# Moving one of six weight loads in the block-product pairs of a decoder layer: up's two-row sum block behind the last blocks of gate and up

## The chip, the cores and the metric

The kernel runs on one core of one Trainium2 chip. The metric is device time in microseconds (us) of one execution, lower is better. A core has TensorE (PE in the profile, with its weight loads as PEld), VectorE (DVE), ScalarE (ACT), GpSimd (POOL), and SyncE (SP), which here only issues transfers. All transfers of the core share 16 DMA engines.

## The reference, cut to what matters

One decoder layer on 512 tokens of width 1024: a half-step SwiGLU feed-forward network (FFN), a token mixing step (a pooling branch beside sliding-window attention, merged by gates), and a second half-step SwiGLU FFN. All in float32.

```python
def swiglu(x, w_gate, w_up, w_down):
    return (jax.nn.silu(x @ w_gate) * (x @ w_up)) @ w_down

h = h + 0.5 * swiglu(rmsnorm(h, ffn1_norm), ffn1_w_gate, ffn1_w_up, ffn1_w_down)
...
h = h + 0.5 * swiglu(rmsnorm(h, ffn2_norm), ffn2_w_gate, ffn2_w_up, ffn2_w_down)
```

`w_gate` and `w_up` are 1024 x 2816, which is 22 column tiles of 128. The change lies in how the products `x @ w_gate` and `x @ w_up` of the two FFNs get their weights.

## The kernel before, in words

**Precision.** Every product is made of three passes over weights and moving data that are split in a high part (rounded to the format that TensorE reads, by ACT) and a low part (the rest, by a subtraction on DVE or POOL): high by high, high by low, low by high. They are lines 544 to 546 for whole tiles and 650 to 652 for blocks.

**Plain tiles and pairs.** The first 8 column tiles of FFN 1 and the first 6 of FFN 2 are computed plainly. The other 14 and 16 are taken two at a time, in 7 and 8 pairs (`PAIRS`). A pair uses a Strassen-Winograd scheme: gate and up each take 7 block products where plain blocks would take 8, so 14 products a pair (`STEPS`). A product is 12 matmuls of 128 columns of weights by 256 tokens, followed by one count on the semaphore `product`. `done(n, i, pos)` is the count that says that product number `pos` (0 to 13) of pair `i` of FFN `n` has ended.

**What a pair needs.** For gate and for up alike:

- `a1` (512 KB, a row of two blocks; `gate_a`, `up_a` in the profile, line 418),
- `s31` (two rows of weights in one 512 KB transfer, line 423), to which POOL adds another 512 KB by an accumulating transfer of its own (`add_units`, line 1463). The result is the two-row sum block. It has two buffers, so it is fetched two pairs ahead. `gate_s`, `up_s` in the profile,
- `a22` (256 KB; also `gate_a`, `up_a`, line 428).

The profile leaves buffer names out: `up_s` is up's `s31`, `s2` or `s4`, and `up_a` is its `a1` or `a22`.

**What is made of them.** DVE adds `s2` and `s4` from `s31` and `a1` (`weight_sums`, lines 1670 and 1672), ACT rounds each block to its high part (lines 1043 to 1057), DVE subtracts the low parts of `a1`, `s2` and `s31` (lines 1678, 1682, 1686), and POOL those of `s4` and `a22` (`late_lows`, lines 1468 and 1471). DVE also adds partial sums of the product banks in PSUM (`add_part`, line 1802), which TensorE's last two products of the pair, `a22(0)` and `a22(1)`, positions 12 and 13, wait for.

**Order.** Each engine runs its own list in the order in which it is written; the semaphores alone tie the lists. SP's list for a pair is `pairs`, with a wait on `product` in front of each load. POOL's list for a pair is the four `late_lows` (gate's s4, gate's a22, up's s4, up's a22), then the two `add_units` of the pair after next, gate's and up's; each `add_units` first waits until the `s31` load that it adds to has landed. DVE's list for a pair is in `pair`: two partial sums, then for the next pair `weight_sums` and `low_a1` of gate (behind product 4), the same of up (behind product 6), `low_s2` of gate, then partial sum, `low_s31` of gate, and three more partial sums.

```python
def add_units(n, i, k, w):
    g = first_pair(n) + i
    pool.wait_ge(w["s31_landed"][buffer(g)], 16 * fills(g))
    pool.dma_start(w["s31"][buffer(g)][:, :], weights_in[D_PAIRS[n] + 4 * i + k + 2, :, :],
                   accum_op=ALU.add).then_inc(w["s31_summed"][buffer(g)], 16)
...
late_lows(first_pair(n) + i, gate_w)
late_lows(first_pair(n) + i, up_w)
if i + 2 < PAIRS[n]:
    add_units(n, i + 2, 0, gate_w)
    add_units(n, i + 2, 1, up_w)
```

Of the kernel before, what the change touches and what calls it, by code (L numbers as in the profile page):

```python
# [55 lines left out]
PAIRS = tuple((FT - p) // 2 for p in PLAIN)  # L56
# [68 lines left out]
def layer_kernel(nc, x_in, consts_in, params_in, poolw_in, weights_in, out):  # L125
    ctx = ExitStack()
    with ctx:
# [4 lines left out]
        def sem(name):  # L132
            return ctx.enter_context(nc.semaphore(name))
# [37 lines left out]
        def blocks(name, a, s31, s2, a22, s4, high_a, high_s31, high_s2, high_a22, high_s4):  # L171

            wide, one = [P, UNIT], [P, UNIT // 2]
            return dict(
                a=put(name + "_a1", wide, a), a_l=put(name + "_a1_low", wide, a, F32R),
                s31=[put(f"{name}_s31_{q}", wide, o) for q, o in enumerate(s31)],
                s31_l=[put(f"{name}_s31_low_{q}", wide, o, F32R) for q, o in enumerate(s31)],
                s2=put(name + "_s2", one, s2), s2_l=put(name + "_s2_low", one, s2, F32R),
                a22=put(name + "_a22", one, a22), a22_l=put(name + "_a22_low", one, a22, F32R),
                s4=[put(f"{name}_s4_{q}", one, o) for q, o in enumerate(s4)],  # L180
                s4_l=[put(f"{name}_s4_low_{q}", one, o, F32R) for q, o in enumerate(s4)],
                a_h=put(name + "_a1_high", wide, high_a, F32R), s31_h=put(name + "_s31_high", wide, high_s31, F32R),
                s2_h=put(name + "_s2_high", one, high_s2, F32R), a22_h=put(name + "_a22_high", one, high_a22, F32R),
                s4_h=put(name + "_s4_high", one, high_s4, F32R),
                a_landed=sem(name + "_a1_landed"), s31_landed=[sem(f"{name}_s31_landed{q}") for q in range(2)],
                s31_summed=[sem(f"{name}_s31_summed{q}") for q in range(2)], a22_landed=sem(name + "_a22_landed"),
                summed=sem(name + "_s2_s4_summed"), high=sem(name + "_blocks_high"),
                low=sem(name + "_blocks_low"), late=sem(name + "_late_blocks_low"))
# [5 lines left out]
        up_w = blocks("up", m, (m + 4096, m + 12288), m + 8192, m + 10240, (M_UP_S4, M_UP_S4 + 2048),  # L194
                      M_HIGH, M_HIGH + 4096, M_HIGH + 8192, M_HIGH + 10240, M_HIGH + 12288)
# [83 lines left out]
        product = sem("product_done")  # L279
# [75 lines left out]
        def first_pair(n):  # L355

            return PAIRS[0] if n else 0

        def buffer(g):

            return (g if g < PAIRS[0] else g - PAIRS[0]) % 2
# [7 lines left out]
        def done(n, i, pos):  # L369

            return STEPS * (first_pair(n) + i) + pos + 1
# [30 lines left out]
        def _(sp):  # L402
# [14 lines left out]
            def load_a1(n, i, k, w):  # L417
                sp.dma_start(w["a"][:, :], weights_in[D_PAIRS[n] + 4 * i + k, :, :]).then_inc(w["a_landed"], 16)

            def load_s31(n, i, k, w):  # L420
                d = D_PAIRS[n] + 4 * i + k
                b = buffer(first_pair(n) + i)
                sp.dma_start(w["s31"][b][:, :].rearrange("p (a n) -> p a n", a=2),
                             weights_in[d:d + 3:2, :, 0:UNIT // 2].rearrange("a p n -> p a n")
                             ).then_inc(w["s31_landed"][b], 16)

            def load_a22(n, i, k, w):
                sp.dma_start(w["a22"][:, :], weights_in[D_PAIRS[n] + 4 * i + k + 2, :, UNIT // 2:UNIT]
                             ).then_inc(w["a22_landed"], 16)
# [18 lines left out]
            def pairs(n):  # L448

                for i in range(PAIRS[n]):  # L450
                    if i + 1 < PAIRS[n]:
                        sp.wait_ge(product, done(n, i, 1))
                        load_a1(n, i + 1, 0, gate_w)
                        sp.wait_ge(product, done(n, i, 3))
                        load_a1(n, i + 1, 1, up_w)
                    if i + 2 < PAIRS[n]:
                        sp.wait_ge(product, done(n, i, 8))
                        load_s31(n, i + 2, 0, gate_w)
                        sp.wait_ge(product, done(n, i, 10))
                        load_s31(n, i + 2, 1, up_w)  # L460
                    if i + 1 < PAIRS[n]:
                        sp.wait_ge(product, done(n, i, 12))
                        load_a22(n, i + 1, 0, gate_w)
                        sp.wait_ge(product, done(n, i, 13))
                        load_a22(n, i + 1, 1, up_w)

            def first_down(n, u):

                last = PAIRS[n] - 1
                sp.wait_ge(product, done(n, last, 3))  # L470
                load(u)
                sp.wait_ge(product, done(n, last, 10))
                load(u + 1)
                sp.wait_ge(product, done(n, last, 13))
                load(u + 2)
                load(u + 3)
# [30 lines left out]
            for u in range(SLOTS, U_DN1):  # L507
                load_used(u)
                if u == SLOTS + 4:
                    gate_prologue(0)  # L510
            up_prologue(0, U_DN1 - SLOTS)
            pairs(0)
            first_down(0, U_DN1)
            for u in range(U_DN1 + SLOTS, U_POOL + SLOTS):
# [5 lines left out]
            for u in range(U_GU2 + SLOTS + 1, U_DN2):  # L520
                load_used(u)
            up_prologue(1, U_DN2 - SLOTS)
            pairs(1)
            first_down(1, U_DN2)
            for u in range(U_DN2 + SLOTS, UNITS):
# [1711 lines left out]
```

## Time and profile before

| what | value |
|---|---|
| median of 3 runs | 1045.54 us (1045.41 to 1046.3) |
| the profiled execution's own time | 1046.29 us |
| its span, first to last instruction | 1044.5 us |
| PE busy | 1037.8 us (99%) |
| PEld busy | 904.9 us (87%) |
| DVE busy | 648.8 us (62%) |
| ACT busy | 469.2 us (45%) |
| POOL busy | 407.6 us (39%) |
| granted TensorE clock | 1.0 |
| read from HBM | 121.76 MB |

The profile is of one execution. Its times are us from the span's start unless marked ns. A row of the timeline gives an instruction's start, how long it took, its engine, its line in the kernel, its operation and its tiles (written, then read), and in brackets the idle time of the engine before it and what ended it. A row of a transfer queue gives packets, MB and the share of the 16 DMA engines' time; a row of single transfers gives the tile, the queue that issues, the count, the size and the us from issue to landing. Transfers of POOL's queue are the accumulating ones. The pairs of FFN 1 lie between 95 and 237 us, those of FFN 2 between 758 and 922 us.

### The profile page before, as it was taken

To read this page: it belongs to the slowest core of one execution; us is meant where nothing else is said; L and a number is where in the kernel's file an instruction comes from. 1 tells how busy PE (TensorE), PEld (TensorE's weight loads), DVE (VectorE), ACT (ScalarE), POOL (GpSimd) and SP (SyncE) were. 2 spreads that over 40 slices of the span, in tenths; PEclk is the share of its full clock that TensorE was granted. 3 is DMA by queue.
4 is the path that set the end of the run, shared out by engine and by line. 5 is a ranking of instruction groups with operands and counts; after the bars stand their busy time and mean duration, and the time that the engine had idled before them with its cause. 6 is when DMAs were issued, how large, how long until landed. Compare 5 with 4: busy or idle time off the path is not lost.

```text
span 1044.5 us, 15205 instructions
## 1 busy us (share of the span) xinstructions
PE 1037.8 (99%) x5940; PEld 904.9 (87%) x5940; DVE 648.8 (62%) x997; ACT 469.2 (45%) x810; POOL 407.6 (39%) x229
## 2 busy tenths in 40 slices
PE   9999999999999999999999999999999999999998
PEld 7888999998888888887777888888899999988887
DVE  6997776669240378426677656679996777594101
ACT  6453554545231334247676643434345554453210
POOL 1302334325444443344455545434324233254441
PEclk9999999999999999999999999999999999999999
DMA  6735677613233432222111122325367577232332
GB/s 212 215 102 133 165 188 195 179 53 120 92 100 101 141 122 84 87 81 81 61 61 60 56 70 97 101 87 146 111 163 193 157 183 195 80 105 98 101 101 101
DMA packets 42292, 124.81 MB, mean 119 GB/s; under 512 B 4336, under 2 KB 5616, under 8 KB 42224
## 3 DMA queue, kind: packets, MB, share of 16 engines
q1 hardware_dynamic: 37616, 107.85, 31.2%
q0 software_dynamic: 4320, 15.73, 8.9%
q8 instruction: 46, 0.75, 0.3%
q10 hardware_dynamic: 288, 0.29, 0.1%
q14 instruction: 22, 0.18, 0.0%
HBM read 121.76 MB, written 2.10 MB: 119 GB/s over the span
## 4 chain that ended last, share of the span: by engine, by line
PE 95%; DVE 2%; DMA 1%; issue 1%; ACT 1%; SPq 0%; DVEq 0%; ACTq 0%
PE psum L544 21%; PE psum L545 21%; PE psum L546 21%; PE psum L650 9%; PE psum L651 9%; PE psum L652 9%; PE psum L904 1%; PE psum L918 1%; DMA gate_a<-weights_dram 1%; PE psum L812 1%; PE psum L931 1%; PE psum L933 1%; PE psum L932 1%; DMA h<-x_dram 0%; ACT probs L1373 0%
## 5 line engine op out<-in xcount | busy, mean ns | idle before, releaser
L1000 ACT ACTIVATE w_high<-w_raw 128x1024 fp32r<-128x1024 f32 x118 | 124.6, 1056 | 229.4 <-DMA w_raw<-weights_dram 181.1
L1457 POOL TENSOR_TENSOR w_low_in_place<-w_raw,w_high 128x1024 fp32r<-128x1024 f32 x59 | 145.7, 2473 | 177.1 <-ACT w_high L1000 177.1
L1457 POOL TENSOR_TENSOR w_low<-w_raw,w_high 128x1024 fp32r<-128x1024 f32 x50 | 122.8, 2457 | 110.5 <-ACT w_high L1000 110.5
L544 PE MATMUL psum<-hidden_high,w_high 128*128 128x512 f32 x350 | 136.2, 389 | 0.0
L545 PE MATMUL psum<-hidden_low,w_high 128*128 128x512 f32 x350 | 136.2, 389 | 0.0
L546 PE MATMUL psum<-hidden_high,w_low_in_place 128*128 128x512 f32 x350 | 136.2, 389 | 0.0
L544 PE MATMUL psum<-u_high,w_high 128*128 128x512 f32 x240 | 97.9, 408 | 0.0
L545 PE MATMUL psum<-u_low,w_high 128*128 128x512 f32 x240 | 93.9, 391 | 0.0
L546 PE MATMUL psum<-u_high,w_low 128*128 128x512 f32 x240 | 93.7, 390 | 0.0
L544 PE MATMUL psum<-ffn_u_high,w_high 128*128 128x512 f32 x222 | 87.3, 393 | 0.3 <-DVE ffn_u_low L1572 0.3
L546 PE MATMUL psum<-ffn_u_high,w_low_in_place 128*128 128x512 f32 x222 | 86.4, 389 | 0.0
L545 PE MATMUL psum<-ffn_u_low,w_high 128*128 128x512 f32 x222 | 86.4, 389 | 0.0
L544 PEld LDWEIGHTS psum<-hidden_high,w_high 128*128 128x128 f32 x350 | 65.7, 188 | 13.7
L546 PEld LDWEIGHTS psum<-hidden_high,w_low_in_place 128*128 128x128 f32 x350 | 65.7, 188 | 13.6
L545 PEld LDWEIGHTS psum<-hidden_low,w_high 128*128 128x128 f32 x350 | 65.7, 188 | 13.5
L1583 DVE SCALAR_TENSOR_TENSOR h<-psum,h 128x512 f32<-128x512 f32 x23 | 15.9, 689 | 95.7 <-PE psum L546 95.7
L1766 DVE TENSOR_TENSOR hidden_low<-hidden,hidden_high 128x512 fp32r<-128x512 f32 x44 | 63.6, 1501 | 13.1 <-ACT hidden_high L1069 13.1
L544 PEld LDWEIGHTS psum<-u_high,w_high 128*128 128x128 f32 x240 | 45.1, 188 | 10.8 <-issue 0.5
L546 PEld LDWEIGHTS psum<-u_high,w_low 128*128 128x128 f32 x240 | 45.1, 188 | 9.9
L1523 POOL TENSOR_TENSOR probs<-probs,inv_denominator 128x1024 f32<-128x1024 f32 (+1 forms) x16 | 26.9, 1681 | 66.4 <-DVE inv_denominator L2043 66.4
L545 PEld LDWEIGHTS psum<-u_low,w_high 128*128 128x128 f32 x240 | 45.1, 188 | 8.7 <-issue 0.5
L650 PE MATMUL psum<-moving_sums_high,up_s_high 128*128 128x256 f32 x180 | 50.9, 283 | 0.0
(270 smaller groups left out, 2820.3 us busy)
## 6 DMA issues: line engine op xcount, KB each, us to landing
w_raw<-weights_dram SPq DMA_DIRECT2D x118, 512.0 KB, 3.5
gate_a<-weights_dram SPq DMA_DIRECT2D x15, 512.0 KB, 6.4
gate_s<-weights_dram SPq DMA_DIRECT2D x15, 512.0 KB, 3.6
gate_s<-weights_dram POOLq DMA_DIRECT2D x15, 512.0 KB, 6.8
up_a<-weights_dram SPq DMA_DIRECT2D x15, 512.0 KB, 4.9
up_s<-weights_dram SPq DMA_DIRECT2D x15, 512.0 KB, 3.6
up_s<-weights_dram POOLq DMA_DIRECT2D x15, 512.0 KB, 8.3
gate_a<-weights_dram SPq DMA_DIRECT2D x15, 256.0 KB, 5.4
```

The source lines that it names most:

```text
L544: pe.matmul(o, wh, xh, start=start, stop=False)
L545: pe.matmul(o, wh, xl, start=False, stop=False)
L546: return pe.matmul(o, wl, xh, start=False, stop=stop)
L650: pe.matmul(o, wh[:, w], xh[:, c, :], start=fresh and c == 0, stop=False, skip_group_check=not fresh)
L651: pe.matmul(o, wh[:, w], xl[:, c, :], start=False, stop=False, skip_group_check=not fresh)
L652: mm = pe.matmul(o, wl[:, w], xh[:, c, :], start=False, stop=c == HALF - 1, skip_group_check=not fresh)
L812: mm = pe.matmul(psum[:, 2, col:col + KV], qsq[:, c % 2, b * BLK:(b + 1) * BLK], head_cols, start=True, stop=True, skip_group_check=True)
L1000: act.activation(high[:, s, :], raw[:, s, :], ACT.Copy).then_inc(high_done, 1)
L1457: pool.tensor_tensor(wlow[:, s, :], raw[:, s, :], high[:, s, :], ALU.subtract).then_inc(low_done, 1)
L1523: pool.tensor_tensor(p, p, rden[:, j % 2, :].unsqueeze(2).to_broadcast([P, 4, width]), ALU.mult).then_inc(probs_ready, 1)
L1583: dve.scalar_tensor_tensor(out=tile(h, c), in0=psum[:, bank, :], scalar=scale, in1=tile(h, c), op0=ALU.mult, op1=ALU.add).then_inc(done, 1)
L1766: dve.tensor_tensor(hid_l[:, f, :], hid[:, f, :], hid_h[:, f, :], ALU.subtract).then_inc(F["hidden_low"], 1)
```

## The change

In `pairs`, SP's load of up's `s31` for the pair after next loses its own wait (`done(n, i, 10)`) and is written behind the loads of gate's and up's `a22`, so behind the wait `done(n, i, 13)`. No other engine's list changes.

```diff
                     if i + 2 < PAIRS[n]:
                         sp.wait_ge(product, done(n, i, 8))
                         load_s31(n, i + 2, 0, gate_w)
-                        sp.wait_ge(product, done(n, i, 10))
-                        load_s31(n, i + 2, 1, up_w)
                     if i + 1 < PAIRS[n]:
                         sp.wait_ge(product, done(n, i, 12))
                         load_a22(n, i + 1, 0, gate_w)
                         sp.wait_ge(product, done(n, i, 13))
                         load_a22(n, i + 1, 1, up_w)
+                    if i + 2 < PAIRS[n]:
+                        load_s31(n, i + 2, 1, up_w)
```

SP's list, a pair of FFN 1 and the start of the next (`up_s_1_97` is up's `s31` buffer 1, `gate_a_83` and `up_a_102` are the `a22` blocks, `gate_a_75` and `up_a_94` are the `a1` blocks):

```order
 L423 DMA gate_s_1_78<-weights_dram 128x2x512
-L423 DMA up_s_1_97<-weights_dram 128x2x512
 L428 DMA gate_a_83<-weights_dram 128x512
 L428 DMA up_a_102<-weights_dram 128x512
+L423 DMA up_s_1_97<-weights_dram 128x2x512
 L418 DMA gate_a_75<-weights_dram 128x1024
 L418 DMA up_a_94<-weights_dram 128x1024
```

One transfer moved past two others. It moves in 5 pairs of FFN 1 and 6 pairs of FFN 2 (11 in all); the last two pairs of each FFN load no `s31`.

POOL's list over the same stretch, which is the same before and after the change (`up_s_0_96` is up's `s31`, buffer 0):

```order
L1463 DMA gate_s_0_77<-weights_dram 128x1024
L1463 DMA up_s_0_96<-weights_dram 128x1024
L1468 TENSOR_TENSOR gate_s_low_88<-gate_s_1_86,gate_s_high 128x512
L1471 TENSOR_TENSOR gate_a_low<-gate_a_83,gate_a_high 128x512
L1468 TENSOR_TENSOR up_s_low_107<-up_s_1_105,up_s_high 128x512
L1471 TENSOR_TENSOR up_a_low<-up_a_102,up_a_high 128x512
```

Nothing moved here, but the second row waits for the transfer that SP now issues later, and the four subtractions stand behind it.

## Rows read from the trace of the kernel before

**Rows 1.** The page: busy us (share of the span) xinstructions, then queues and transfers.

```profile
PE 1037.8 (99%) x5940; PEld 904.9 (87%) x5940; DVE 648.8 (62%) x997; ACT 469.2 (45%) x810; POOL 407.6 (39%) x229
...
q1 hardware_dynamic: 37616, 107.85, 31.2%
q0 software_dynamic: 4320, 15.73, 8.9%
...
up_s<-weights_dram SPq DMA_DIRECT2D x15, 512.0 KB, 3.6
up_s<-weights_dram POOLq DMA_DIRECT2D x15, 512.0 KB, 8.3
```

**Rows 2.** Timeline of SP's queue around one pair boundary of FFN 1.

```profile
171.71 0.38 SPq L423 DMA_DIRECT2D up_s<-weights_dram  x1
174.59 0.34 SPq L428 DMA_DIRECT2D gate_a<-weights_dram  x1
176.03 0.34 SPq L428 DMA_DIRECT2D up_a<-weights_dram  x1
178.91 0.33 SPq L418 DMA_DIRECT2D gate_a<-weights_dram  x1
```

**Rows 3.** The same, later pairs: the load behind the last product.

```profile
196.19 0.34 SPq L428 DMA_DIRECT2D up_a<-weights_dram  x1
216.87 0.33 SPq L428 DMA_DIRECT2D up_a<-weights_dram  x1
840.69 0.34 SPq L428 DMA_DIRECT2D up_a<-weights_dram  x1
861.04 0.34 SPq L428 DMA_DIRECT2D up_a<-weights_dram  x1
881.79 0.34 SPq L428 DMA_DIRECT2D up_a<-weights_dram  x1
```

**Rows 4.** The chain that ended last, 213 to 216 us: start, us, what.

```profile
214.70 0.34 DVE up L1802
215.17 0.36 PE psum L650
```

**Rows 5.** Timeline of DVE: weight sums, gate's first in four pairs, up's in one.

```profile
185.02 1.31 DVE L1670 TENSOR_TENSOR gate_s<-gate_s,gate_a 128x512 f32<-128x512 f32 x1 [2.80 <-DMA gate_a<-weights_dram]
188.31 0.69 DVE L1670 TENSOR_TENSOR up_s<-up_s,up_a 128x512 f32<-128x512 f32 x1
...
205.79 1.78 DVE L1670 TENSOR_TENSOR gate_s<-gate_s,gate_a 128x512 f32<-128x512 f32 x1 [1.84 <-DMA gate_a<-weights_dram]
851.06 0.69 DVE L1670 TENSOR_TENSOR gate_s<-gate_s,gate_a 128x512 f32<-128x512 f32 x1 [4.18 <-DMA gate_a<-weights_dram]
871.04 1.45 DVE L1670 TENSOR_TENSOR gate_s<-gate_s,gate_a 128x512 f32<-128x512 f32 x1 [2.98 <-DMA gate_a<-weights_dram]
```

**Rows 6.** Timeline of POOL: the last of its four subtractions, pair from 175.8.

```profile
184.49 1.30 POOL L1471 TENSOR_TENSOR up_a_low<-up_a,up_a_high 128x512 fp32r<-128x512 f32 x1 [1.67 <-ACT up_a_high L1057]
```

**Rows 7.** Timeline of POOL and DVE in the first pair of FFN 2.

```profile
763.06 1.61 POOL L1468 TENSOR_TENSOR gate_s_low<-gate_s,gate_s_high 128x512 fp32r<-128x512 f32 x1
766.83 1.58 POOL L1471 TENSOR_TENSOR up_a_low<-up_a,up_a_high 128x512 fp32r<-128x512 f32 x1
...
763.86 5.12 DVE L1621 SCALAR_TENSOR_TENSOR gate<-tanh,gate 128x512 f32<-128x512 f32 x1 [0.64 <-ACT tanh L1029]
```

**Rows 8.** Single transfers, issued 174.59; 98.89, 100.93; 762.50, 764.35: us to landing.

```profile
gate_a<-weights_dram SPq DMA_DIRECT2D x1, 256.0 KB, 4.8
...
up_s<-weights_dram POOLq DMA_DIRECT2D x1, 512.0 KB, 7.9
up_a<-weights_dram SPq DMA_DIRECT2D x1, 512.0 KB, 6.8
...
up_s<-weights_dram POOLq DMA_DIRECT2D x1, 512.0 KB, 6.0
up_a<-weights_dram SPq DMA_DIRECT2D x1, 512.0 KB, 5.5
```

## The prediction

> **What bounds the kernel now.** The page's busy line comes first: TensorE is busy for 1037.8 us of the span, 99% [rows 1]. Only what makes TensorE wait can cost time, and only the waits it has now can be gained. The next view is the timeline of SP's queue, because SP issues a load when a block product has ended, and so shows the beat of the pairs. Call O the moment at which SP issues up's a22, just behind product 13; for the model pair O is 176.03 [rows 2]. The next O is 196.19 [rows 3], so a pair without a wait takes 20.16 us, and a product 1.44 us. The pair after that has its O at 216.87: 20.68, which is 0.52 more. In FFN 2 the O's 840.69, 861.04 and 881.79 are 20.35 and 20.75 apart: 0.19 and 0.59 too much [rows 3]. In the other eight of the 11 pairs whose weight sums the moved load feeds (pairs 1 to 5 of FFN 1 and 1 to 6 of FFN 2), the same distances are 20.16. So these 11 pairs hold **1.30 us** of waits in all.
>
> What makes those waits? The chain of waits has, in the pair with 0.52, DVE's partial sum of up (line 1802) ending at 215.04 and TensorE's next matmul at 215.17 [rows 4]. That is product 13, which needs the sum. DVE does this sum at the end of a closed queue: gate's weight sums, up's weight sums, low parts, partial sums, one behind the other. So what counts is when the head of that queue, gate's first weight sum, ends, measured from O. From [rows 5] with the O's of [rows 2, 3]:
>
> - 186.33 - 176.03 = 10.30: no wait
> - 851.75 - 840.69 = 11.06: 0.19
> - 207.57 - 196.19 = 11.38: 0.52
> - 872.49 - 861.04 = 11.45: 0.59
>
> The wait is the excess over **O + 10.87**, us for us. Up's first sum starts at 188.31, 1.98 behind the end of gate's [rows 5], so the same limit for up's sum is O + 12.85.
>
> **The change, part by part.** No instruction is added or removed. One 512 KB transfer moves in each of 11 pairs, from 171.71 in the model pair to behind up's a22: 176.03 + 0.34 = 176.37 [rows 2]. Everything else follows from that.
>
> *What it passes on SP's queue.* Gate's and up's a22 are no longer behind 512 KB and up's accumulate; they can only come earlier. Nobody on TensorE's path waits for them today, so I cost that at nothing. Gate's a1, issued at 178.91, now stands behind the moved load and ahead of up's accumulate instead of beside it. It can land 3.6 after its issue (the median of a load that runs alone, [rows 1]), 182.5 or O + 6.5, where today gate's first sum waits for it until O + 9. That is the gain the change offers, and its ceiling is the 1.30 us above.
>
> *When the moved load lands.* Not before 3.6 behind its issue [rows 1]: 179.97, O + 3.9. The upper bound: gate's a22, issued 174.59, lands 4.8 later at 179.39 today [rows 8], late because of accumulates; up's a22 and the moved load then follow at the engines' rate. The hardware queue took 31.2% of 1044.5 us for 107.85 MB [rows 1], 1.6 us for 512 KB and 0.8 for 256 KB: 181.8, O + 5.7. I take the middle, **O + 4.8**, since one of the two accumulates that delay today's a22 is gone from there.
>
> *What waits for it.* POOL's list is in order: the accumulate for up waits for the load, and the four subtractions of s4 and a22 wait behind it. Today they are strewn over DVE's quiet time; in the model pair the last one starts at 184.49 and ends at 185.79, after a gap of 1.67 [rows 6]. From now on they start about 0.6 behind O + 4.8 (the accumulate issued at 762.50 [rows 8] has its first subtraction at 763.06 [rows 7]), so at O + 5.4, and run back to back, since their inputs are there by then. TensorE wants the first of them at product 9, O + 13, and it is done by O + 7: that by itself costs nothing.
>
> *What they do to DVE.* Gate's weight sum becomes ready behind product 4, at O + 7.2, in the middle of the four. DVE's sum of 0.69 us took 1.31 while POOL's last subtraction ran, and ended 0.54 behind it [rows 5, 6]. Worse, in the first pair of FFN 2 an operation of DVE with two inputs in SBUF took 5.12 us: it started at 763.86, amid four back-to-back subtractions from 763.06, and ended at 768.98, 5.92 behind the start of the first [rows 7]. If gate's sum is shut out like that, it ends at O + 5.4 + 5.9 = O + 11.3, a wait of 0.43. If DVE gets its turn after one subtraction, gate's sum ends at O + 8.5, the two operations behind it lose up to 1.26 each ((766.83 - 763.06) / 3, [rows 7]), and the queue stands as if it had ended at O + 11.0 at most: a wait of 0 to 0.13. I take the middle of 0.43 and 0.07, **0.25 us a pair**; the ends, with the load's bounds, are 0 and 11.3 + 0.9 - 10.87 = 1.3.
>
> The Trainium skill ("SBUF — State Buffer", section "SBUF: two separate sides") says that the port pair shared by VectorE and GpSimd is an exclusive lock, which the instruction that starts first holds to its end. By that rule alone the operation of 5.12 us should have waited for one subtraction, not four, and the sum would be 0 to 0.13 us a pair; the row goes beyond the rule, so I keep both.
>
> *The accumulate and up's a1.* The accumulate is issued at O + 4.8, where today it can go 3.6 behind 171.71, about O - 0.7 [rows 1, 2]. With nothing but loads of SP beside it, such an accumulate took 6.0 in one place and 7.9 in another, and up's a1 landed 1.35 and 0.94 behind it (764.35 + 5.5 against 768.5; 100.93 + 6.8 against 106.79) [rows 8]. So up's sums could start at O + 12.15 or at O + 13.6, against the limit O + 12.85. With the first this costs nothing, with the second 0.75. The accumulating queue's 8.9% over 30 transfers is 3.1 us of all engines each [rows 1], so even the median today, 8.3 [rows 1], holds waits for others that are now gone; I take the shorter and keep 7.9 for the range.
>
> *Sum.* 11 pairs x 0.25 = 2.75, less the 1.30 of waits in them today: **+1.45 us** on the profiled execution's 1046.29. The median of the runs is 0.75 lower, at 1045.54, and I make the forecast against it: 1047.0. About 0.2%, 2.1 us, is what a measurement can tell from no change; this is below it.
>
> **The rivals.**
>
> *A. The forecast*: waits of 0.12 to 0.31 in a pair, net 0 to +2.1, 1045.5 to 1047.6. For it: the new head of the queue falls within half a microsecond of the limit on all reckonings. Chance 0.40.
>
> *B. Slower: up's accumulate comes too late.* Place: DVE's weight sum of up. Price: with 7.9 us for the accumulate, 0.75 x 11 - 1.3 = +7, 1052.5; it decides from 7.2 us on (O + 4.8 + 7.2 + 0.9 = O + 12.9). Being shut out (0.43 x 11 - 1.3 = +3.4, 1049) gives the milder form. For it: the trace has both the long accumulate and the shutting out [rows 7, 8]. Against: both rows are of first pairs, where DVE also has work of the plain tiles. Chance 0.38 for +2.1 to +8. The Trainium skill ("DMA: Bandwidth & Descriptors", section "SWDGE vs HWDGE vs iDMA") says that a DMA engine takes turns between its software and hardware queues; by it up's a1 would not be held until the accumulate is through. The 5.5 and 6.8 us against 3.6 speak rather for being held.
>
> *C. No waits left.* DVE gets its turn between the subtractions and the shorter accumulate holds; the 1.3 us are gained in part or whole: 1044.2 to 1045.5. Chance 0.14.
>
> *D. Worse*: the load lands at its upper bound and DVE is shut out as well: 1.3 x 11 - 1.3 = +13, 1058.5. Against: the lateness of today's a22 goes with the accumulate that it competes with. Chance 0.05.
>
> *E. Nothing happens*, because the load was already late at its old place: against it stands its issue at 171.71 right behind product 10 [rows 2]. Chance 0.03.
>
> **How the numbers follow.** Same: A, C and E, 0.57, of which I give 0.01 to each side for the edges. Slower: B and D, 0.43. A gain over 2.1 us needs more waits than there are. The range: from 1044.3 (C) to 1053.0, which leaves out D, the end of B and the last of C. A alone is 1045.5 to 1047.6.
>
> **What would show it.** In the changed profile the moved load is issued 0.3 behind up's a22 and lands at O + 3.9 to 5.7; gate's a1 lands near O + 6.5; POOL's four subtractions lie without gaps from about O + 5.4 to O + 10.5; gate's first weight sum on DVE takes well over 1 us; up's accumulate lands between O + 10.8 and O + 12.7. The distances between O's give the wait of each pair. The prediction is wrong if these distances exceed 20.5 on average (then B or D), or if the moved load lands late enough that TensorE waits for a low part of s4 itself.

## The result: 14.0 us slower, and the profile after

| | before | changed |
|---|---|---|
| median of 4 runs | 1045.47 us (1045.1 to 1046.3) | 1059.45 us (1058.21 to 1060.56) |
| ratio to before | 1 | 1.0132 (95% interval 1.012 to 1.0144) |
| the profiled execution, its span | 1046.29, 1044.5 us | 1058.21, 1056.4 us |

The forecast was 1047.0 with a range of 1044.3 to 1053.0. The change costs 14 us, near the price of rival D (1058.5), which had a chance of 0.05. The profiled executions are 11.9 us apart, since the changed kernel's is the fastest of its four. What follows accounts for these 11.9; the rest of the 14.0 has no trace.

Below, each ratio is to the kernel before, run in the same session as the experiment. Its median was 1045.72 us beside split_after, split_before, hold_subtractions and behind_12; 1046.3 beside gap_after_add, no_up_add, gap_and_late_a1 and before_pair0; and 1046.89 beside satisfied_wait, hold_with_dma and pair0_again. Ratios of different sessions can be compared, medians only roughly.

The page of the changed kernel gives the busy us of each engine. Its groups then give line 1670 on DVE (count, then busy us and mean ns of one, then the idle time before it):

```profile
PE 1041.2 (99%) x5940; PEld 905.7 (86%) x5940; DVE 687.3 (65%) x997; ACT 469.6 (44%) x810; POOL 407.5 (39%) x229
...
L1670 DVE TENSOR_TENSOR gate_s<-gate_s,gate_a 128x512 f32<-128x512 f32 x15 | 54.8, 3653 | 12.7 <-DMA gate_a<-weights_dram 6.7
```

The same group in the kernel before, from its groups by line and form:

```profile
L1670 DVE TENSOR_TENSOR gate_s<-gate_s,gate_a 128x512 f32<-128x512 f32 x15 | 16.1, 1071 | 32.2 <-DMA gate_a<-weights_dram 32.2
```

DVE's busy time rose by 38.5 us (648.8 before, [rows 1]), and gate's first weight sum alone rose by 38.7. It does not do more; it is listed as running while POOL's subtractions shut it out. TensorE's count of matmuls is the same.

What waits for whom on TensorE in the changed kernel (us in total, times, longest):

```profile
PE psum L650 <- DVE gate L1802: 7.9, 9, 1.7
PE psum L578 <- DVE sum_of_squares L1566: 1.5, 1, 1.5
```

The first row is new. Line 1802 holds the partial sums that products 12 and 13 need, as in [rows 4]. The list shows only the longer waits; the distances between O's (the issue of up's a22) give them all. Minus 20.16 each, they are, for the 11 pairs: 2.01, 0.34, 1.05, 1.59, 0.99 in FFN 1 and 1.27, 1.59, 1.20, 1.16, 2.29, 0.05 in FFN 2: **13.5 us**, against 1.30 before. The difference, 12.2, accounts for the 11.9 between the spans.

SP's queue in one pair (O is 179.20), to compare with [rows 2]:

```profile
177.39 0.33 SPq L428 DMA_DIRECT2D gate_a<-weights_dram  x1
179.20 0.33 SPq L428 DMA_DIRECT2D up_a<-weights_dram  x1
179.57 0.53 SPq L423 DMA_DIRECT2D up_s<-weights_dram  x1
182.08 0.33 SPq L418 DMA_DIRECT2D gate_a<-weights_dram  x1
```

POOL and DVE behind it, to compare with [rows 5, 6]:

```profile
185.16 0.86 POOL L1463 DMA_DIRECT2D up_s<-weights_dram  x1 [9.43 <-DMA up_s<-weights_dram]
185.72 1.62 POOL L1468 TENSOR_TENSOR gate_s_low<-gate_s,gate_s_high 128x512 fp32r<-128x512 f32 x1
186.99 1.60 POOL L1471 TENSOR_TENSOR gate_a_low<-gate_a,gate_a_high 128x512 fp32r<-128x512 f32 x1
188.24 1.60 POOL L1468 TENSOR_TENSOR up_s_low<-up_s,up_s_high 128x512 fp32r<-128x512 f32 x1
189.50 1.59 POOL L1471 TENSOR_TENSOR up_a_low<-up_a,up_a_high 128x512 fp32r<-128x512 f32 x1
```

```profile
186.40 5.25 DVE L1670 TENSOR_TENSOR gate_s<-gate_s,gate_a 128x512 f32<-128x512 f32 x1 [1.01 <-PE psum L652]
...
193.62 0.68 DVE L1670 TENSOR_TENSOR up_s<-up_s,up_a 128x512 f32<-128x512 f32 x1
```

The chain of waits at the end of that pair:

```profile
198.76 0.34 DVE up L1802
199.11 0.14 issue
199.24 0.36 PE psum L650
```

The moved load landed at O + 5.68, and POOL, after waiting 9.43 us, issued the accumulate 0.29 later, at O + 5.96. Then it ran its four subtractions without a gap. DVE's sum, 0.69 us when nothing hinders it, is listed from 186.40, inside the first of them, to 191.65, behind the last. Its end at O + 12.45 is 1.58 over the limit of O + 10.87, and the wait of this pair was 1.59. The same reckoning holds to 0.01 in ten of the 11 pairs; only in the last of FFN 1's five did up's a1, landed at O + 13.7, set a longer wait (0.99) than the sum (0.45).

### The profile page after: what moved, and what is told of

The parts are those of the page before. It is cut to its first block, busy times and chain, and to the rows that moved or that the text cites. A ratio compares the mean times of both kernels' runs of the same rounds, so it can differ in the third digit from the quotient of the medians.

```text
span 1056.4 us, 15205 instructions
## 1 busy us (share of the span) xinstructions
PE 1041.2 (99%) x5940; PEld 905.7 (86%) x5940; DVE 687.3 (65%) x997; ACT 469.6 (44%) x810; POOL 407.5 (39%) x229
## 4 chain that ended last, share of the span: by engine, by line
PE 86%; DVE 7%; DMA 3%; issue 2%; ACT 1%; DVEq 0%; ACTq 0%
PE psum L544 21%; PE psum L546 20%; PE psum L545 20%; PE psum L650 7%; PE psum L652 6%; PE psum L651 6%; DVE gate_s L1670 3%; DMA gate_a<-weights_dram 2%; PE psum L904 1%; PE psum L918 1%; DMA up_a<-weights_dram 1%; PE psum L812 1%; DVE up_s L1672 1%; DVE up_s L1670 1%; PE psum L931 1%
## 5 line engine op out<-in xcount | busy, mean ns | idle before, releaser
L1457 POOL TENSOR_TENSOR w_low_in_place<-w_raw,w_high 128x1024 fp32r<-128x1024 f32 x59 | 145.9, 2476 | 175.8 <-ACT w_high L1000 175.7
L1463 POOL DMA_DIRECT2D up_s<-weights_dram x15 | 13.0, 865 | 167.9 <-DMA up_s<-weights_dram 167.9
L544 PEld LDWEIGHTS psum<-hidden_high,w_high 128*128 128x128 f32 x350 | 65.7, 188 | 13.7
L545 PEld LDWEIGHTS psum<-hidden_low,w_high 128*128 128x128 f32 x350 | 65.7, 188 | 13.7
L1670 DVE TENSOR_TENSOR gate_s<-gate_s,gate_a 128x512 f32<-128x512 f32 x15 | 54.8, 3653 | 12.7 <-DMA gate_a<-weights_dram 6.7
```

The lines of the kernel that those rows point to most:

```text
L544: pe.matmul(o, wh, xh, start=start, stop=False)
L545: pe.matmul(o, wh, xl, start=False, stop=False)
L1457: pool.tensor_tensor(wlow[:, s, :], raw[:, s, :], high[:, s, :], ALU.subtract).then_inc(low_done, 1)
L1670: dve.tensor_tensor(w["s2"][:, :], s1, w["a"][:, 0:UNIT // 2], ALU.add).then_inc(w["summed"], 1)
```

## The experiments

The theories that the texts below name: **1 or L**, DVE is shut out by four back-to-back subtractions; **2**, the accumulate or up's a1 is late; **R**, a refinement found on the way, that the shutting out belongs to subtractions that stand right behind a DMA issue of POOL.

### A first group of four

**split_after** (on the changed kernel) and **split_before** (on the kernel before): up's accumulate goes between gate's two and up's two subtractions.

```diff
                     late_lows(first_pair(n) + i, gate_w)
+                    if i and i + 1 < PAIRS[n]:
+                        add_units(n, i + 1, 1, up_w)
                     late_lows(first_pair(n) + i, up_w)
                     if i + 2 < PAIRS[n]:
                         add_units(n, i + 2, 0, gate_w)
-                        add_units(n, i + 2, 1, up_w)
```

> The changed kernel, but POOL issues up's accumulate between gate's two subtractions and up's two, one pair-step later in its list, so gate's two no longer wait for the moved load. O is the issue of up's a22. Theory 1 (DVE's first weight sum of gate is shut out by four back-to-back subtractions): only up's two subtractions, about O+7 to O+9.7, can shut it out; it ends at about O+10.2, under the limit O+10.87, and most of the 13.5 us of waits go: 1046 to 1050. Theory 2 (the lateness of up's accumulate or of up's a1 sets the waits): the accumulate is issued at about O+6.3, later than the O+5.2 of the changed kernel, and lands at O+12.3 to O+14; the waits stay or grow: 1058 to 1066.

> The kernel before (load at its old place) with the same new place of up's accumulate on POOL: between gate's two and up's two subtractions. Theory 1: no wait from subtractions, as four back-to-back never stand over gate's sum; whatever waits there are come from the accumulate issued at O+6.3. Theory 2: same waits as in the other kernel with this POOL order, since the accumulate is issued at the same time in both. Both: within 1 us of the other one if the place of the load itself does not matter once POOL's list is not held by it. If gate's a1 landing early is worth something, at or below 1045.5.

Measured: split_after 1055.03 us, ratio 1.0093 (1.0076 to 1.0109); split_before 1056.58, ratio 1.0097 (1.008 to 1.0114). Neither theory had the number of split_after. In both, gate's first sum ends by O + 10.72 in each of the 11 pairs, under the limit, as theory 1 said. But most of the 13.5 us of waits stayed, 9.8 and 11.1 in the 11 pairs, where theory 1 had most of them go and theory 2 had all of them stay. In split_before, in a pair whose O is 829.07, DVE's rows are:

```profile
836.29 3.13 DVE L1671 TENSOR_TENSOR gate_s<-gate_s,gate_a 128x512 f32<-128x512 f32 x1 [1.02 <-PE psum L652]
...
843.45 0.69 DVE L1671 TENSOR_TENSOR up_s<-up_s,up_a 128x512 f32<-128x512 f32 x1 [1.97 <-PE psum L652]
```

Gate's sum ended at O + 10.35. DVE then idled 1.97 us, and up's first sum started at O + 14.4, 0.13 behind the landing of up's accumulate, issued at O + 6.35. (The row names product 6 as the releaser; it had ended 4 us before.) So an accumulate issued at O + 6 costs about 10 us on its own, with the load where it always was. The two mechanisms are parallel: taking one away bares the other.

**hold_subtractions** (on the kernel before) moves no transfer, only the subtractions:

```diff
                 for i in range(PAIRS[n]):
+                    if i and i + 1 < PAIRS[n]:
+                        pool.wait_ge(product, done(n, i, 3))
                     late_lows(first_pair(n) + i, gate_w)
```

> The kernel before, with all transfers where they were, but in the 11 pairs POOL waits for product 3 in front of its four subtractions, so that they run back to back from about O+5.9 as in the changed kernel. Theory 1: gate's first sum is shut out until about O+5.9+5.9=O+11.8 in each pair, a wait of 0.9 us, 11 x 0.9 - 1.3 = +8 to +10: 1054 to 1056. Theory 2: no transfer is moved, so 1045 to 1047.

Measured: 1049.06, ratio 1.0033 (1.002 to 1.0045), waits of 2.9 us in the 11 pairs. That is a loss of 3.3 where theory 1 wanted 8 to 10, and the 11 pairs hold only 1.6 us more of waits than before. (Another 1.1 lies in FFN 1's first pair, which this edit leaves alone; see the clean test.) The rows, POOL and then DVE (O is 822.66), say why:

```profile
830.99 1.30 POOL L1468 TENSOR_TENSOR up_s_low<-up_s,up_s_high 128x512 fp32r<-128x512 f32 x1
832.24 1.74 POOL L1471 TENSOR_TENSOR up_a_low<-up_a,up_a_high 128x512 fp32r<-128x512 f32 x1
```

```profile
831.50 1.33 DVE L1672 TENSOR_TENSOR gate_s<-gate_s,gate_a 128x512 f32<-128x512 f32 x1 [2.65 <-DMA gate_a<-weights_dram]
832.87 1.67 DVE L1674 TENSOR_TENSOR gate_s<-gate_s,gate_a 128x512 f32<-128x512 f32 x1
```

DVE waited for the third subtraction alone and then had its turn; the fourth waited for DVE (1.74 where the third took 1.30). Four back-to-back subtractions do not by themselves shut DVE out. Something else must stand ahead of them where they do.

**behind_12**: the load at an intermediate place.

```diff
-                        sp.wait_ge(product, done(n, i, 10))
-                        load_s31(n, i + 2, 1, up_w)
                     if i + 1 < PAIRS[n]:
                         sp.wait_ge(product, done(n, i, 12))
+                        if i + 2 < PAIRS[n]:
+                            load_s31(n, i + 2, 1, up_w)
```

> The load of up's two-row block behind product 12, ahead of gate's a22, 1.8 us earlier than in the changed kernel. It should land about O-1.4+3.7, O+2.3, so POOL's four subtractions start near where they do before (O+3.2 to O+5). Theory 1: gate's first sum is not shut out for four; 1044.5 to 1047. Theory 2: the accumulate is issued at O+2.3 and lands at O+8.3 to O+11, earlier than the limit too; 1044.5 to 1047. It tells how steep the step between the two places is: a loss over 4 us here would speak against both.

Measured: 1050.09, ratio 1.0039 (1.0025 to 1.0053), a loss of some 4 us; a miss for both. The waits alternate: 0, 1.24, 0, 0.81, 0 in FFN 1 and 0.10, 0, 2.00, 0, 1.29, 0 in FFN 2, 5.4 us in all. Behind a pair with a wait, the load is issued at O - 1.8 and lands at O + 2.1 to O + 4.0; behind most pairs without one it is issued at O - 1.44 and lands at O + 4.5 to O + 5.4, gate's accumulate being under way until O + 2.0 to O + 2.4 (until O + 0.6 to O + 1.6 behind a pair with a wait). So a wait at the end of a pair gives gate's accumulate a head start and spares the next pair; that this alone sets the alternation was not tested.

### A second group: what shuts DVE out

In all 11 pairs of the changed kernel, and in FFN 2's first pair before [rows 7], the first subtraction starts 0.56 to 0.57 us behind the issue of an accumulate by POOL. In hold_subtractions it starts behind a wait. That is theory R.

**gap_after_add** (on the changed kernel):

```diff
                 for i in range(PAIRS[n]):
+                    if i and i + 1 < PAIRS[n]:
+                        pool.wait_ge(product, done(n, i, 4))
                     late_lows(first_pair(n) + i, gate_w)
```

> The changed kernel, but in the 11 pairs POOL waits for product 4 between up's accumulate and its four subtractions, which therefore start later than in the changed kernel, at about O+7.3, and end at about O+12.8. Theory R (DVE is shut out only by subtractions that POOL starts right behind its own DMA issue, where each is listed as 1.6 us with starts 1.26 apart; behind a wait on a semaphore they are listed as 1.29 and DVE gets in between two of them): gate's first sum ends by O+8.6 and both its sums by O+10.5; up's sum is then bound by the accumulate alone, some 6 to 7 us of waits: 1050 to 1052. Theory L (any four back-to-back subtractions shut DVE out): gate's first sum ends at O+13.1, 2.2 us over the limit in each pair: 1068 or more.

Measured: 1061.09, ratio 1.0148 (1.0129 to 1.0166). POOL, then DVE, O 829.66:

```profile
835.72 0.86 POOL L1463 DMA_DIRECT2D up_s<-weights_dram  x1 [9.39 <-DMA up_s<-weights_dram]
836.92 1.29 POOL L1468 TENSOR_TENSOR gate_s_low<-gate_s,gate_s_high 128x512 fp32r<-128x512 f32 x1 [0.33 <-PE psum L652]
838.18 1.74 POOL L1471 TENSOR_TENSOR gate_a_low<-gate_a,gate_a_high 128x512 fp32r<-128x512 f32 x1
```

```profile
837.37 1.38 DVE L1672 TENSOR_TENSOR gate_s<-gate_s,gate_a 128x512 f32<-128x512 f32 x1 [1.52 <-DMA gate_a<-weights_dram]
838.79 1.68 DVE L1674 TENSOR_TENSOR gate_s<-gate_s,gate_a 128x512 f32<-128x512 f32 x1
840.57 2.13 DVE L1680 TENSOR_TENSOR gate_a_low<-gate_a,gate_a_high 128x1024 fp32r<-128x1024 f32 x1
```

With a pause of 0.33 us, DVE's sum takes 1.38 us and not 3.7 to 5.5 as in the changed kernel, although the subtractions start later. R is right about the sum, which ended between O + 7.9 and O + 9.1 in all 11 pairs. The time is wrong in both expectations: the 11 pairs hold 15.0 us of waits. In four of them the accumulate sets the wait by itself. It lands at O + 14.06 to O + 15.18, up's first sum starts 0.12 behind it, and that start less the limit of O + 12.85 is the wait (1.34, 1.34, 2.46 and 1.93). In the other seven the four subtractions now collide one after another with DVE's busy stretch: its second sum takes 1.68 and not 0.69, its low part 2.13 and not 1.23, and so on to the fourth, which ends at O + 14.2 or later. Two pairs had their accumulate by O + 10.5 and still waited 0.99. The pause ends the shutting out, but neither the collisions nor the late accumulate.

**satisfied_wait**: the same wait instruction, on product 2, which has ended long before.

> The changed kernel with a wait of POOL between up's accumulate and the subtractions that is already met when POOL comes to it (product 2, ended at O+4.3). If it is the pause behind the DMA issue that lets DVE in, and not the wait instruction, nothing changes: 1058 to 1061, gate's first sum over 3.5 us in most pairs. If the wait instruction itself helps, the sum is under 2 us, and the time as in gap_after_add or lower.

Measured: 1060.13, ratio 1.013 (1.0114 to 1.0145); line group of gate's first sum:

```profile
L1672 DVE TENSOR_TENSOR gate_s<-gate_s,gate_a 128x512 f32<-128x512 f32 x15 | 55.7, 3713 | 12.1 <-PE psum L652 9.1 <-DMA gate_a<-weights_dram 2.9
```

That is as in the changed kernel, and the first subtraction again starts 0.56 behind the issue in all 11 pairs. It is the pause that counts, not the instruction.

**no_up_add** leaves up's accumulates out, so that up's two-row sum block lacks its second part; POOL waits for the load as before.

```diff
                 pool.wait_ge(w["s31_landed"][buffer(g)], 16 * fills(g))
-                pool.dma_start(w["s31"][buffer(g)][:, :], weights_in[D_PAIRS[n] + 4 * i + k + 2, :, :],
-                               accum_op=ALU.add).then_inc(w["s31_summed"][buffer(g)], 16)
+                if k == 0:
+                    pool.dma_start(w["s31"][buffer(g)][:, :], weights_in[D_PAIRS[n] + 4 * i + k + 2, :, :],
+                                   accum_op=ALU.add).then_inc(w["s31_summed"][buffer(g)], 16)
```

(ACT and DVE wait for up's `s31_landed` in place of `s31_summed`.)

> The changed kernel without up's accumulating transfers (the second row is not added to up's two-row block, so the output differs). POOL still waits for the moved load in front of its four subtractions, so these stand where they do in the changed kernel or 0.3 earlier. Theory R: no DMA issue of POOL stands ahead of them, DVE gets in, and nothing is late: 1044 to 1046. Theory L: gate's first sum is shut out as before, ends about O+12: 1055 to 1059. Theory 2 (only the accumulate counts): 1044 to 1046 too, but it is told from R by the duration of gate's first sum: above 3.5 us under L, under 2 us under R.

Measured: 1044.89, ratio 0.9989 (0.998 to 0.9999). POOL, then DVE, O 839.75:

```profile
845.22 1.28 POOL L1469 TENSOR_TENSOR gate_s_low<-gate_s,gate_s_high 128x512 fp32r<-128x512 f32 x1 [7.97 <-DMA up_s<-weights_dram]
846.47 1.28 POOL L1472 TENSOR_TENSOR gate_a_low<-gate_a,gate_a_high 128x512 fp32r<-128x512 f32 x1
```

```profile
846.96 1.34 DVE L1671 TENSOR_TENSOR gate_s<-gate_s,gate_a 128x512 f32<-128x512 f32 x1 [1.02 <-PE psum L652]
```

The moved load landed at O + 4.9 to O + 7.1 and the subtractions stood where they do in the changed kernel; the 13.5 us of waits shrank to 2.1, and gate's first sum took 0.86 to 1.85 us. So neither the place of the load nor that of the subtractions costs 14 us. The accumulate does, in two ways: by coming late, and by what its issue does to the instructions behind it.

**gap_and_late_a1**: gap_after_add, and up's a1 behind product 5 in pairs from the second on (`done(n, i, 5 if i else 3)`).

> As gap_after_add, and in the same pairs SP issues up's a1 behind product 5 in place of 3, at O+8.6, so that it no longer competes with the accumulate. If the accumulate takes 7 to 8 us because up's a1 is issued within a microsecond of it, it should now take about 5.5 and land at O+10.5 to O+11.5, and a1 at about O+12.2, under the limit of O+12.85: waits under 1 us in all, 1044 to 1046. If its length has another cause, it stays at 7 to 8 and the time at 1050 to 1052.

Measured: 1059.93, ratio 1.013 (1.0114 to 1.0147), a miss. The accumulate did get shorter, 5.8 us from issue to landing in the mean of the 11 pairs against 7.6 in gap_after_add, so an a1 issued within a microsecond of it stretches it on average. (Not each time: in two pairs of gap_after_add, with a1 0.91 behind, it took 5.4 and 5.6.) The time did not follow: the collisions stayed, and up's a1 itself now landed at O + 12.1 to O + 14.3. In two pairs POOL came to the wait late, with the accumulate issued at O + 6.5; POOL, then DVE, in one of them:

```profile
187.08 0.86 POOL L1463 DMA_DIRECT2D up_s<-weights_dram  x1 [9.86 <-DMA up_s<-weights_dram]
187.86 1.42 POOL L1468 TENSOR_TENSOR gate_s_low<-gate_s,gate_s_high 128x512 fp32r<-128x512 f32 x1
```

```profile
188.13 5.45 DVE L1672 TENSOR_TENSOR gate_s<-gate_s,gate_a 128x512 f32<-128x512 f32 x1 [1.34 <-DMA gate_a<-weights_dram]
```

The subtraction starts 0.78 behind the issue, and DVE is shut out again (the other such pair: 0.74 and 5.44 us). In the nine other pairs of this kernel the subtraction starts 1.07 to 2.01 behind, and DVE gets in.

### The clean test

**hold_with_dma**: hold_subtractions, which moves no transfer and lets DVE in, plus one tiny DMA.

```diff
                         pool.wait_ge(product, done(n, i, 3))
+                        pool.dma_start(pad[:, 6:8], params_in[:, 0:2]).then_inc(pad_landed, 16)
                     late_lows(first_pair(n) + i, gate_w)
```

(POOL also waits, ahead of the wait shown, for the tiny transfer of the pair before.)

> hold_subtractions (no transfer moved, four subtractions behind product 3) with one addition: right behind that wait POOL issues a tiny transfer of 8 bytes a partition into unused memory, and then the subtractions. Theory R: the subtractions now start about 0.57 behind a DMA issue and are listed as 1.6 us; DVE is shut out to the end of the fourth, so gate's first sum ends near O+12.0 where it ended by O+9.9 to O+10.3, each pair waits about 1.1, 11 x 1.1 - 1.3 = +11: 1055 to 1058. Against R: the subtractions only start 0.6 later, DVE gets in as in hold_subtractions: 1049 to 1051.

Measured: 1062.74, ratio 1.0152 (1.0137 to 1.0168). POOL, then DVE, O 181.59:

```profile
187.89 0.57 POOL L1492 DMA_DIRECT2D pad<-params_dram  x1 [7.54 <-PE psum L654]
188.47 1.32 POOL L1470 TENSOR_TENSOR gate_s_low<-gate_s,gate_s_high 128x512 fp32r<-128x512 f32 x1
189.72 1.32 POOL L1473 TENSOR_TENSOR gate_a_low<-gate_a,gate_a_high 128x512 fp32r<-128x512 f32 x1
190.98 1.30 POOL L1470 TENSOR_TENSOR up_s_low<-up_s,up_s_high 128x512 fp32r<-128x512 f32 x1
192.24 1.30 POOL L1473 TENSOR_TENSOR up_a_low<-up_a,up_a_high 128x512 fp32r<-128x512 f32 x1
```

```profile
189.13 4.96 DVE L1680 TENSOR_TENSOR gate_s<-gate_s,gate_a 128x512 f32<-128x512 f32 x1 [1.35 <-DMA gate_a<-weights_dram]
```

By the ratios, eight bytes a partition cost 12.4 us over hold_subtractions (1.0152 against 1.0033), and the 11 pairs hold 14.8 us more of waits in the traces. Gate's first sum ends at O + 12.50 in ten of the 11 pairs, each of which then waits 1.64, the excess over O + 10.87. The expectation was some 5 us short, because the subtractions start 1.06 us later than in hold_subtractions, not 0.6, and so end at O + 11.9. (The later start is not what shuts DVE out: in gap_after_add they start later still, at O + 7.3, and DVE gets in.) It also named a sign that failed: the subtractions are listed as 1.3 us here, not 1.6, and shut DVE out all the same. What counts is that they start right behind a DMA issue, whatever the DMA carries.

A comparison that nobody set up supports this. In FFN 1's first pair the start of the first subtraction behind POOL's issue varies from one execution to the next. The pair in the kernel before, then in split_before, which does not touch it:

```profile
98.89 0.86 POOL L1463 DMA_DIRECT2D up_s<-weights_dram  x1 [9.98 <-DMA up_s<-weights_dram]
99.72 1.37 POOL L1468 TENSOR_TENSOR gate_s_low<-gate_s,gate_s_high 128x512 fp32r<-128x512 f32 x1
100.98 1.91 DVE L1621 SCALAR_TENSOR_TENSOR gate<-tanh,gate 128x512 f32<-128x512 f32 x1 [1.14 <-ACT tanh L1029]
```

```profile
98.97 0.86 POOL L1463 DMA_DIRECT2D up_s<-weights_dram  x1 [9.94 <-DMA up_s<-weights_dram]
99.70 1.45 POOL L1468 TENSOR_TENSOR gate_s_low<-gate_s,gate_s_high 128x512 fp32r<-128x512 f32 x1
100.97 4.49 DVE L1622 SCALAR_TENSOR_TENSOR gate<-tanh,gate 128x512 f32<-128x512 f32 x1 [1.15 <-ACT tanh L1029]
```

At 0.83 DVE got in (1.91 us), at 0.73 it was shut out (4.49). Ten of the 13 traces leave the first pairs and their order as they were: in four the distance is 0.83, 0.84, 0.90 and 1.07 and DVE's operation took 1.83 to 1.91 us; in six it is 0.56 to 0.78 and it took 4.43 to 4.68. In those six the distance from this O to the next is 26.9 to 27.2 us, in the four 25.8 to 26.0. So the kernel before meets the fault by chance in FFN 1 and in its trace in FFN 2, and about 1 us of any comparison here can be this chance.

### A version that beats both

**before_pair0** and **pair0_again** are one kernel: the kernel before with a pause in the first pair of each FFN, the place where it can have the fault itself.

```diff
                 for i in range(PAIRS[n]):
+                    if i == 0:
+                        pool.wait_ge(product, done(n, i, 3))
                     late_lows(first_pair(n) + i, gate_w)
```

> The kernel before, with one wait more: in pair 0 of each FFN, POOL waits for product 3 between its accumulate and the subtractions. Theory R: the operation of DVE of 5.12 us in FFN 2 shrinks to under 2, gate's first sum of that pair starts some 2 us earlier, and 1.0 to 1.4 us of waits at its end go: 1044.2 to 1044.6, a ratio of 0.9988. Theory L: the subtractions start 1.1 later and shut DVE out just as long or longer: 1045.5 to 1047.

> The kernel of before_pair0 once more, to narrow its ratio to the kernel before: 0.9988 to 0.9992, 1044.6 to 1045.0 against about 1045.6.

Measured: 1045.07, ratio 0.999 (0.9981 to 0.9999); again 1044.9, ratio 0.9983 (0.9974 to 0.9992). POOL, then DVE, FFN 2's first pair, to compare with [rows 7]:

```profile
761.78 0.86 POOL L1463 DMA_DIRECT2D up_s<-weights_dram  x1 [9.97 <-DMA up_s<-weights_dram]
763.82 1.29 POOL L1468 TENSOR_TENSOR gate_s_low<-gate_s,gate_s_high 128x512 fp32r<-128x512 f32 x1 [1.18 <-PE psum L652]
```

```profile
763.26 0.69 DVE L1623 SCALAR_TENSOR_TENSOR gate<-tanh,gate 128x512 f32<-128x512 f32 x1 [0.57 <-ACT tanh L1029]
763.98 1.67 DVE L1629 TENSOR_TENSOR hidden<-up,gate 128x512 f32<-128x512 f32 x1
```

The operation of 5.12 us takes 0.69. The kernel is faster by 0.1 to 0.2% (1 to 2 us), and both intervals lie below 1. In the two traces the distance from this pair's O to the next is 1.12 us shorter. FFN 1's first pair is 0.66 and 0.90 longer than in the trace before, where DVE had got in anyway. The 11 later pairs hold 0.03 and 0.13 of waits in place of 1.30, though the pause does not touch them, and why is not known. So the mended pair is shown, and the size of the whole gain only in part.

## Why the prediction was wrong, point by point

- **The head of DVE's queue and its limit, O + 10.87, us for us**: right. It gives the wait of every pair of the changed kernel but one, and of hold_with_dma to 0.01. The 1.30 us of waits before were read rightly too. Gate's a1 did land earlier (O + 6.4 to O + 7.6, where it was O + 7.6 to O + 10.3), but none of the gain that this offered came through.
- **When the moved load lands, O + 3.9 to O + 5.7, taken as O + 4.8**: mis-sized. It landed at O + 4.1 to O + 6.4, in the mean 5.3. Each 0.1 us here is 0.1 in each pair.
- **From the load's landing to the accumulate's issue**: put at nothing, without a reason. It was 0.29 us in each pair.
- **What the subtractions do to DVE**: the step that failed. I put the middle, 0.25, between being shut out (0.43) and taking turns (0.07), as if chance decided. Gate's sum was shut out in 11 pairs of 11, because the first subtraction started 0.56 behind the accumulate's issue each time. The row of 5.12 us [rows 7] showed just this order of instructions, and I read only the four subtractions in it. With the three terms as they were, the sum closes: 5.27 to the landing, 0.29 to the issue, 0.56 to the first subtraction and 5.93 to the end of gate's sum, less 10.87, is 1.18 a pair; with the 0.54 that up's a1 added in one pair that is the 13.5 us. Taking turns was too cheap as well: in hold_subtractions seven of the 11 pairs waited 0.27 to 0.29, not 0 to 0.13.
- **The rule of the Trainium skill** ("SBUF — State Buffer", section "SBUF: two separate sides"), that whichever of the two engines starts first holds the shared port pair for that instruction: it fits hold_subtractions (1.33 and 1.74 us, each waiting for one instruction of the other), and not the 3.7 to 5.5 us behind a DMA issue. The measurement goes beyond the rule.
- **The accumulate, 6.0 with 7.9 kept for the range**: the longer one was typical. From issue to landing it took 7.0 to 8.7 us in nine of the 11 pairs and 5.3 and 5.7 in the two where it was issued over 1 us ahead of up's a1. Rival B's mechanism is real. An estimate from the landings of the accumulate and of a1 in this trace, less O + 12.85 and summed, is 6 to 7 us of waits here had DVE not been shut out; split_before shows it alone, with an issue at O + 6, at +10.
- **The sum**: 11 pairs were right, 0.25 should have been 1.23. Rival D had both of the causes, a late load and DVE shut out. Its +13 is close partly by luck: it took the load at O + 5.7 where the mean was 5.3, and left the 0.29 out. Its chance of 0.05 was the error, since the shutting out was certain here.

## What to carry to other kernels

Look at what stands behind a wait in an in-order list before moving what it waits for: here one load held an accumulate and four unrelated subtractions, made the accumulate late, and put the subtractions right behind its issue in DVE's busiest time. Where a short DVE operation is listed at several times its length (here 5.25 us for 0.69), look at the whole run of GpSimd instructions around it, the DMA issue in front included. Where DVE's turn matters, try a pause between a GpSimd DMA issue and GpSimd arithmetic: in before_pair0 it let DVE in and paid. In gap_after_add it let DVE in and did not pay, because the later start made new collisions.

## What the runs showed of the hardware that was not expected

- Subtractions of POOL that start 0.56 to 0.78 us behind its DMA issue ran back to back through a waiting DVE operation with two SBUF inputs, up to 5.46 us. Starting 0.83 us or more behind, or behind a semaphore wait alone, they let it in after one at most. This holds in all 13 traces (the nearest cases on both sides: 0.78 in behind_12 and gap_and_late_a1, 0.83 in the kernel before). In one pair of behind_12 that began 0.56 behind, the run itself broke off for some 0.3 us, and DVE got in there (1.84 us). It holds for a transfer of 8 bytes a partition. What in POOL does this is not shown.
- An accumulating transfer of 512 KB took 5.8 us in the mean when the next load of SP was issued 2.1 to 3.4 us behind it (gap_and_late_a1), and 7.6 when that load was issued within a microsecond of it, before or behind (gap_after_add).
